# Delta rule's block stage: 16x16 diagonal blocks stored by eight transfers per tile, query products evicted by VectorE

## The chip, the cores and the metric

The kernel runs on one core of a Trainium2 chip. Its time is the device time of one execution in microseconds; a version's time is the median of its runs. The engines are TensorE (PE; its weight loads PEld), VectorE (DVE), ScalarE (ACT), GpSimd (POOL) and SyncE (SP), which issues most of the DMA transfers.

## What is computed

The reference is one inference step through two trunk layers of a hybrid backbone. The second layer holds a chunked gated delta rule. Of that the change touches the products and the inverses of small blocks:

```python
kb = kc * bc[..., None]
a_mat = jnp.where(strict, jnp.einsum('nbhid,nbhjd->nbhij', kb, kc) * gamma, 0.0) + jnp.eye(C_CHUNK)
sol = lax.linalg.triangular_solve(a_mat, rhs, left_side=True, lower=True)
attn = jnp.where(tri, jnp.einsum('nbhid,nbhjd->nbhij', qc, kc) * gamma, 0.0)
```

The kernel works on chunks of 128 tokens. The products of keys with keys (`kk`) and of queries with keys (`qk`) do not depend on the direction of the scan; gamma and beta do. The triangular system is solved by inverting its 16x16 diagonal blocks first and joining them later.

## The kernel before

`delta_net` (not far above the functions shown) runs four stages one after the other: `delta_prepare`, `delta_blocks`, `delta_chunks`, `delta_outputs`. Each is a `Stage` with its own buffers, and ends with a barrier of all engines. The change is in `delta_blocks` alone (its buffers are named `gdna_...` in the profile).

There are NT = 9 tiles of P = 128 tokens, 8 heads, blocks of BASE = 16, so NB = 8 blocks per tile. `delta_blocks` works as follows.

TensorE first turns the gates `gc` and `beta` (L2808, L2809). ScalarE copies them to `rows` (128 rows) and `rest` (16 rows), SyncE stores these four pieces (L2777, L2778), waits for them, and loads them back in another order as `gcb` and `bb` (L2781). Then for each tile t TensorE makes 8 products for `kk` into a PSUM tile `pk[t % 2]` and 8 for `qk` into `pq[t % 2]` (L2819). ScalarE evicts both (L2835), each a 128x1024 tile of 512 KB, into two alternating buffers of each. VectorE multiplies `kk` with a mask of the blocks, `own`, into `cut` (L2856), and sums over the blocks into `diag` (L2860), 128 rows by 8 heads by 16 columns: for each row only the 16 columns of its own block. SyncE's queue holds, tile after tile and in this order, the transfers of `diag` (L2784), `kk` (L2786) and `qk` (L2788) to scratch in HBM, each behind a wait for its producer.

Besides, after tile 2 VectorE subtracts `gcb` from itself across rows and columns into `E_` (L2863), and after tile 3 ScalarE makes the absolute value and the exponential of it (L2838, L2840).

When all of `diag` has landed (L2790), SyncE loads it back as `M` (L2792), in two halves, with one block of 16x16 in each partition and tile. VectorE multiplies it by `E_` (L2868) and by `bb` (L2871), inverts the blocks in 30 dependent steps of growing width (L2877, L2878), and makes the transpose `X` of the result (L2879). SyncE stores both as `inv` (L2797). The next stage, `delta_chunks`, reads `kk`, `qk` and `inv` back from HBM.

Transfers of other stages that the prediction looks at: `new_state` (L2961), four of 64 rows, each with four pieces of 256 B, strided at both ends; `moe_rowgp` (L2248), four in a row, of 32 rows of 1 KB; `front_cols` (L1141), of 64 rows of 4 B.

Of the kernel before, what the change touches and what calls it, by code (L numbers as in the profile page):

```python
# [10 lines left out]
ALU = mybir.AluOpType  # L11
ACT = mybir.ActivationFunctionType
AX = mybir.AxisListType

P = 128
# [5 lines left out]
NT = T // P  # L21
# [2547 lines left out]
HEADS = 8  # L2569
HALF = P // 2  # L2570
BASE = 16
NB = P // BASE
# [160 lines left out]

def own_block(a, own):

    return (a.rearrange("p h (b c) -> p h b c", c=BASE),
            own.rearrange("p (o b u) -> p o b u", o=1, u=1).broadcast_to([P, HEADS, NB, BASE]))


def delta_blocks(nc, io, keep, m):

    QT, KT, gc, beta, own = (m[x] for x in ("QT", "KT", "gc", "beta", "own"))
    with Stage(nc, "gdna") as s:
        kk = [s.sb(f"kk{i}", [P, HEADS, P]) for i in range(2)]
        qk = [s.sb(f"qk{i}", [P, HEADS, P]) for i in range(2)]
        cut = s.sb("cut", [P, HEADS, P])
        diag = [s.sb(f"diag{i}", [P, HEADS, BASE]) for i in range(2)]
        rows = s.sb("rows", [P, 2, P])  # L2750
        rest = s.sb("rest", [ROWS - P, 2, P])
        gcb = s.sb("gcb", [P, NT, BASE])
# [6 lines left out]
        pk = [s.ps(f"pk{i}", [P, HEADS, P]) for i in range(2)]  # L2759
        pq = [s.ps(f"pq{i}", [P, HEADS, P]) for i in range(2)]  # L2760
        row_turned, row_taken, row_out = s.sem("row_turned"), s.sem("row_taken"), s.sem("row_out")
        kk_mm, qk_mm, kk_taken, qk_taken = s.sem("kk_mm"), s.sem("qk_mm"), s.sem("kk_taken"), s.sem("qk_taken")
        cut_done, diag_done = s.sem("cut_done"), s.sem("diag_done")
        kk_out, qk_out, diag_out = ([s.sem(f"{n}{i}") for i in range(2)] for n in ("kk_out", "qk_out", "diag_out"))
        gcb_in, bb_in, M_in = s.sem("gcb_in"), s.sem("bb_in"), s.sem("M_in")
        E_done, E_step, Y_set, M_step, solve, inv_out = (s.sem(n) for n in ("E_done", "E_step", "Y_set", "M_step", "solve", "inv_out"))
        inv_done = s.sem("inv_done")
        blk = s.block()
        by_head = lambda a: a[:].rearrange("p (j r) i -> p r j i", r=2)
        by_bank = lambda a: a[:].rearrange("p (r j) i -> p r j i", r=2)  # L2770
        half = P // 2

        @blk.sync
        def _(sp):
            for i, name in enumerate(("gcT", "betaT")):
                sp.wait_ge(row_taken, i + 1)
                sp.dma_start(io[name][0:P, :], rows[:, i, :]).then_inc(row_out, 16)  # L2777
                sp.dma_start(io[name][P:ROWS, :], rest[:, i, :]).then_inc(row_out, 16)  # L2778
            sp.wait_ge(row_out, 64)
            for dst, name, done in ((gcb, "gcT", gcb_in), (bb, "betaT", bb_in)):  # L2780
                sp.dma_start(dst[:], io[name].rearrange("(t r) (b i) -> (r b) t i", t=NT, i=BASE)).then_inc(done, 16)  # L2781
            for t in range(NT):
                sp.wait_ge(diag_done, t + 1)
                sp.dma_start(io["diag"][t].rearrange("h p c -> p h c"), diag[t % 2][:]).then_inc(diag_out[t % 2], 16)  # L2784
                sp.wait_ge(kk_taken, t + 1)
                sp.dma_start(io["kk"][t], kk[t % 2][:]).then_inc(kk_out[t % 2], 16)  # L2786
                sp.wait_ge(qk_taken, t + 1)
                sp.dma_start(io["qk"][t], qk[t % 2][:]).then_inc(qk_out[t % 2], 16)  # L2788
            for i in range(2):
                sp.wait_ge(diag_out[i], 16 * len(range(i, NT, 2)))  # L2790
            for d in range(2):
                sp.dma_start(M[half * d:half * d + half].rearrange("p t i c -> p t (i c)"),  # L2792
                             io["diag"].rearrange("t h (b i) c -> (h b) t (i c)", i=BASE)).then_inc(M_in, 16)
            sp.wait_ge(inv_done, 1)
            for w, parts in enumerate(((X, Y), (Y, X))):
                for d in range(2):
                    sp.dma_start(io["inv"][w].rearrange("(t d h) (b i) c -> d (h b) t (i c)", t=NT, d=2, i=BASE)[d],  # L2797
                                 parts[d][half * d:half * d + half].rearrange("p t i c -> p t (i c)")).then_inc(inv_out, 16)
            for i in range(2):
                sp.wait_ge(kk_out[i], 16 * len(range(i, NT, 2)))  # L2800
                sp.wait_ge(qk_out[i], 16 * len(range(i, NT, 2)))
            sp.wait_ge(inv_out, 64)

# [18 lines left out]
        @blk.scalar  # L2822
        def _(act):
            for i in range(2):
                act.wait_ge(row_turned, i + 1)
                nc.scalar.activation(rows[:, i, :], pk[i][:, 0, :], ACT.Copy)
                nc.scalar.activation(rest[:, i, :], pk[i][0:ROWS - P, 4, :], ACT.Copy).then_inc(row_taken, 1)
            for t in range(NT):
                for dst, bank, mm, out, taken in ((kk, pk, kk_mm, kk_out, kk_taken), (qk, pq, qk_mm, qk_out, qk_taken)):
                    act.wait_ge(mm, t + 1)  # L2830
                    if t >= 2:
                        act.wait_ge(out[t % 2], 16 * (t // 2))
                        if dst is kk:
                            act.wait_ge(cut_done, t - 1)
                    nc.scalar.activation(by_head(dst[t % 2]), by_bank(bank[t % 2]), ACT.Copy).then_inc(taken, 1)  # L2835
                if t == 3:
                    act.wait_ge(E_done, 1)
                    nc.scalar.activation(E_[:], E_[:], ACT.Abs).then_inc(E_step, 1)  # L2838
                    act.wait_ge(E_step, 1)
                    nc.scalar.activation(E_[:], E_[:], ACT.Exp, scale=-1.0).then_inc(E_step, 1)  # L2840
# [8 lines left out]
        @blk.vector  # L2849
        def _(dve):  # L2850
            for t in range(NT):
                dve.wait_ge(kk_taken, t + 1)
                if t:
                    dve.wait_ge(diag_done, t)
                a, mask = own_block(kk[t % 2][:], own[:])
                nc.vector.tensor_tensor(cut[:].rearrange("p h (b c) -> p h b c", c=BASE), a, mask, ALU.mult).then_inc(cut_done, 1)  # L2856
                dve.wait_ge(cut_done, t + 1)
                if t >= 2:
                    dve.wait_ge(diag_out[t % 2], 16 * (t // 2))
                nc.vector.tensor_reduce(diag[t % 2][:], cut[:].rearrange("p h (b c) -> p h c b", c=BASE), axis=AX.X, op=ALU.add).then_inc(diag_done, 1)  # L2860
                if t == 2:
                    dve.wait_ge(gcb_in, 16)
                    nc.vector.tensor_tensor(E_[:], gcb[:].unsqueeze(3).broadcast_to([P, NT, BASE, BASE]),  # L2863
                                            gcb[:].unsqueeze(2).broadcast_to([P, NT, BASE, BASE]), ALU.subtract).then_inc(E_done, 1)
# [10 lines left out]
            for i in range(1, BASE):  # L2875
                p = prod[:, 0:NT * i * i].rearrange("p (t c j) -> p t c j", t=NT, c=i)
# [533 lines left out]
```

## Time and profile before

| | us |
|---|---|
| median of 3 runs | 4162.95 |
| the runs | 4156.73, 4162.95, 4169.68 |
| the profiled execution, its own time | 4168.26 |
| its span in the trace | 4166.5 |
| busy PE / DVE / ACT / POOL | 3579.7 / 2356.5 / 1697.6 / 580.3 |

The trace is of one execution. Times in it count from the start of the span. `delta_blocks` lies at about 2655 to 2762 us of it. "SPq" is SyncE's queue; the number beside one of its entries is the time that issuing the transfer took it, and the landing is told separately, in us from the issue to the last byte. A wait is written as the one who waits, an arrow, and who released it.

### The profile page before, as it was taken

To read this page: it belongs to the slowest core of one execution; us is meant where nothing else is said; L and a number is where in the kernel's file an instruction comes from. 1 tells how busy PE (TensorE), PEld (TensorE's weight loads), DVE (VectorE), ACT (ScalarE), POOL (GpSimd) and SP (SyncE) were. 2 spreads that over 40 slices of the span, in tenths; PEclk is the share of its full clock that TensorE was granted. 3 is DMA by queue.
4 is the path that set the end of the run, shared out by engine and by line. 5 is a ranking of instruction groups with operands and counts; after the bars stand their busy time and mean duration, and the time that the engine had idled before them with its cause. 6 is when DMAs were issued, how large, how long until landed. Compare 5 with 4: busy or idle time off the path is not lost. (4 is left out here: it accounts for less than half of the span.)

```text
span 4166.5 us, 56312 instructions
## 1 busy us (share of the span) xinstructions
PE 3579.7 (86%) x22440; PEld 2693.4 (65%) x22440; DVE 2356.5 (57%) x3625; ACT 1697.6 (41%) x2573; POOL 580.3 (14%) x467
## 2 busy tenths in 40 slices
PE   6979787997769999997999886439996689999995
PEld 1469755665646666664999764439995556666663
DVE  5163333334568787785514443645555668778884
ACT  2031154002346566563211266424434256656563
POOL 0020131221000010000200000026541101000000
PEclk8989898998879999998999997759997899999997
DMA  4142385414448888885443202333316458888885
GB/s 163 66 141 80 109 284 176 130 58 152 177 165 298 297 281 284 292 289 187 144 115 93 113 11 89 109 85 100 93 49 202 157 214 289 283 287 295 298 279 198
DMA packets 378504, 743.15 MB, mean 178 GB/s; under 512 B 99512, under 2 KB 222535, under 8 KB 377080
## 3 DMA queue, kind: packets, MB, share of 16 engines
q1 hardware_dynamic: 358906, 682.76, 47.2%
q0 software_dynamic: 16720, 56.41, 5.5%
q8 instruction: 178, 2.92, 0.3%
q10 hardware_dynamic: 2618, 0.40, 0.1%
q14 instruction: 82, 0.67, 0.0%
HBM read 634.01 MB, written 106.10 MB: 178 GB/s over the span
## 5 line engine op out<-in xcount | busy, mean ns | idle before, releaser
L2482 DVE TENSOR_TENSOR moe_w_low<-ffn_w,moe_w_high 128x1024 fp32r<-128x1024 f32 x768 | 898.9, 1220 | 77.0 <-ACT moe_w_high L2408 74.5
L2408 ACT ACTIVATE moe_w_high<-ffn_w 128x1024 fp32r<-128x1024 f32 x768 | 780.2, 1053 | 221.8 <-DMA ffn_w<-moe_w_gate 130.0
L2332 PE MATMUL moe_small<-ffn_w,ffn_xpT 128*16 128x512 f32 x2048 | 238.3, 594 | 0.0
L2312 PE MATMUL moe_G<-moe_w_high,moe_xT_high 128*128 128x512 f32 x512 | 185.4, 443 | 20.0 <-DVE moe_xT_low L2446 13.3
L224 PE MATMUL proj_mm<-proj_hT_low,proj_w_high 128*128 128x384 f32 x576 | 193.2, 335 | 0.0
L224 PE MATMUL proj_mm<-proj_hT_high,proj_w_low 128*128 128x384 f32 x576 | 193.1, 335 | 0.0
L224 PE MATMUL proj_mm<-proj_hT_high,proj_w_high 128*128 128x384 f32 x576 | 193.1, 335 | 0.0
L224 PE MATMUL proj_mm<-proj_w_high,proj_hT_high 128*128 128x416 f32 (+1 forms) x504 | 178.3, 354 | 11.7 <-POOL proj_hT_low L344 8.6
L3006 PE MATMUL gdnc_a<-gdnc_T,gdnc_kg 128*128 128x64 f32 (+1 forms) x864 | 102.1, 267 | 88.7 <-ACT gdnc_T L3056 86.5
L224 PE MATMUL proj_mm<-proj_w_high,proj_hT_low 128*128 128x416 f32 (+1 forms) x504 | 177.1, 351 | 0.0
L224 PE MATMUL proj_mm<-proj_w_low,proj_hT_high 128*128 128x416 f32 (+1 forms) x504 | 176.0, 349 | 0.0
L2261 POOL DMA_INDIRECT scratch_x<-moe_ys,keep_slot_s x32 | 50.5, 1579 | 867.3 <-DVE moe_ys L2475 867.3
L2312 PE MATMUL moe_Y<-moe_w_high,moe_hT_high 128*128 128x512 f32 x512 | 167.7, 409 | 0.0
L2312 PE MATMUL moe_G<-moe_w_low,moe_xT_high 128*128 128x512 f32 x512 | 161.9, 398 | 0.0
L2436 DVE TENSOR_SCALAR moe_xT<-moe_turn,keep_coef 128x128 f32<-128x128 f32 x248 | 84.8, 404 | 135.9 <-PE moe_turn L2288 135.9
L2312 PE MATMUL moe_G<-moe_w_high,moe_xT_low 128*128 128x512 f32 x512 | 160.0, 394 | 0.0
L2312 PE MATMUL moe_Y<-moe_w_low,moe_hT_high 128*128 128x512 f32 x512 | 159.9, 394 | 0.0
L2312 PE MATMUL moe_U<-moe_w_high,moe_xT_high 128*128 128x512 f32 x512 | 159.7, 393 | 0.0
L2312 PE MATMUL moe_Y<-moe_w_high,moe_hT_low 128*128 128x512 f32 x512 | 159.6, 393 | 0.0
L2312 PE MATMUL moe_U<-moe_w_low,moe_xT_high 128*128 128x512 f32 x512 | 159.3, 392 | 0.0
L2312 PE MATMUL moe_U<-moe_w_high,moe_xT_low 128*128 128x512 f32 x512 | 158.5, 391 | 0.0
L3006 PEld LDWEIGHTS gdnc_a<-gdnc_T,gdnc_kg 128*128 128x128 f32 (+1 forms) x864 | 92.9, 182 | 95.3 <-issue 93.9
(480 smaller groups left out, 7390.8 us busy)
## 6 DMA issues: line engine op xcount, KB each, us to landing
ffn_w<-moe_w_gate SPq DMA_DIRECT2D x256, 512.0 KB, 6.3
ffn_w<-moe_w_up SPq DMA_DIRECT2D x256, 512.0 KB, 7.1
ffn_w<-moe_w_down SPq DMA_DIRECT2D x256, 512.0 KB, 5.8
attnrun_m_w<-w_ada SPq DMA_DIRECT2D x40, 1024.0 KB, 11.3
scratch_conv<-proj_zf POOLq DMA_DIRECT2D x24, 512.0 KB, 2.9
scratch_tm<-proj_tm SPq DMA_DIRECT2D x45, 208.0 KB, 2.1
scratch_spec<-front_room SPq DMA_DIRECT2D x36, 256.0 KB, 2.1
proj_w_raw<-even_w_in SPq DMA_DIRECT2D x24, 384.0 KB, 4.2
```

The source lines that it names most:

```text
L224: mm = nc.tensor.matmul(out, lhs(a, k), rhs(b, k), start=first and n == 0, stop=last and n == len(passes) - 1)
L2261: nc.gpsimd.indirect_dma_start(out=io["x"][l], out_offset=bass.IndirectOffsetOnAxis(ap=rows, axis=0), in_=src[e % 2][:], in_offset=None, c ...
L2312: mm = nc.tensor.matmul(bank[:, half, :], stat[a][:, k, :], cut[b][:, half * BANK:(half + 1) * BANK], start=k == 0 and i == 0, stop=k == K ...
L2332: nc.tensor.matmul(out, stat, w, start=k == 0, stop=k == KD - 1, tile_position=(0, 32 * q)).then_inc(small_done, 1)
L2408: nc.scalar.activation(w_high[n % CUT_ROOM][:], raw_rows(wall, n), ACT.Copy).then_inc(w_up, 1)
L2436: ins = nc.vector.tensor_scalar(xT[:, k, :], turned(k, e), co[:, 0, k:k + 1], co[:, 1, k:k + 1], ALU.mult, ALU.add)
L2482: nc.vector.tensor_tensor(w_low[n % CUT_ROOM][:], raw_rows(wall, n), w_high[n % CUT_ROOM][:].bitcast(F32), ALU.subtract).then_inc(w_cut, 1)
L3006: mm = nc.tensor.matmul(quad(ba[hg])[later, h, :], kg[n % 3][:, 4 * hg + h, later], earlier(Tm[n % 2][:, 4 * hg + h, :], li, d), start=Tru ...
```

## The change

ScalarE evicts `kk` alone, and all nine tiles of it have room of their own. VectorE evicts `qk`, into two buffers as before, behind a wait for the transfer of two tiles earlier. The mask and the sum on VectorE are gone, and `cut` and `diag` with them. In place of the transfer of `diag`, SyncE issues eight transfers per tile straight from the evicted `kk`: for block b the 16 rows and, in each head, the 16 columns of the block, 16 rows of 8 pieces of 64 B. They stand ahead of the transfer of `kk` and wait for its eviction. All count on one semaphore, and `M` is loaded when all 72 have landed. ScalarE's two steps on `E_` stand after tile 4 in place of tile 3.

```diff
@@ def delta_blocks
-        kk = [s.sb(f"kk{i}", [P, HEADS, P]) for i in range(2)]
+        kk = s.sb("kk", [P, NT, HEADS, P])
         qk = [s.sb(f"qk{i}", [P, HEADS, P]) for i in range(2)]
-        cut = s.sb("cut", [P, HEADS, P])
-        diag = [s.sb(f"diag{i}", [P, HEADS, BASE]) for i in range(2)]
@@ SyncE
             for t in range(NT):
-                sp.wait_ge(diag_done, t + 1)
-                sp.dma_start(io["diag"][t].rearrange("h p c -> p h c"), diag[t % 2][:]).then_inc(diag_out[t % 2], 16)
                 sp.wait_ge(kk_taken, t + 1)
-                sp.dma_start(io["kk"][t], kk[t % 2][:]).then_inc(kk_out[t % 2], 16)
+                for b in range(NB):
+                    of_block = slice(b * BASE, (b + 1) * BASE)
+                    sp.dma_start(io["diag"][t, :, of_block, :].rearrange("h p c -> p h c"), kk[of_block, t, :, of_block]).then_inc(diag_out, 16)
+                sp.dma_start(io["kk"][t], kk[:, t]).then_inc(kk_out, 16)
                 sp.wait_ge(qk_taken, t + 1)
                 sp.dma_start(io["qk"][t], qk[t % 2][:]).then_inc(qk_out[t % 2], 16)
-            for i in range(2):
-                sp.wait_ge(diag_out[i], 16 * len(range(i, NT, 2)))
+            sp.wait_ge(diag_out, 16 * NB * NT)
@@ ScalarE
             for t in range(NT):
-                for dst, bank, mm, out, taken in ((kk, pk, kk_mm, kk_out, kk_taken), (qk, pq, qk_mm, qk_out, qk_taken)):
-                    act.wait_ge(mm, t + 1)
-                    if t >= 2:
-                        act.wait_ge(out[t % 2], 16 * (t // 2))
-                        if dst is kk:
-                            act.wait_ge(cut_done, t - 1)
-                    nc.scalar.activation(by_head(dst[t % 2]), by_bank(bank[t % 2]), ACT.Copy).then_inc(taken, 1)
-                if t == 3:
+                act.wait_ge(kk_mm, t + 1)
+                nc.scalar.activation(by_head(kk[:, t]), by_bank(pk[t % 2]), ACT.Copy).then_inc(kk_taken, 1)
+                if t == 4:
@@ VectorE
             for t in range(NT):
-                dve.wait_ge(kk_taken, t + 1)
-                if t:
-                    dve.wait_ge(diag_done, t)
-                a, mask = own_block(kk[t % 2][:], own[:])
-                nc.vector.tensor_tensor(cut[:].rearrange("p h (b c) -> p h b c", c=BASE), a, mask, ALU.mult).then_inc(cut_done, 1)
-                dve.wait_ge(cut_done, t + 1)
+                dve.wait_ge(qk_mm, t + 1)
                 if t >= 2:
-                    dve.wait_ge(diag_out[t % 2], 16 * (t // 2))
-                nc.vector.tensor_reduce(diag[t % 2][:], cut[:].rearrange("p h (b c) -> p h c b", c=BASE), axis=AX.X, op=ALU.add).then_inc(diag_done, 1)
+                    dve.wait_ge(qk_out[t % 2], 16 * (t // 2))
+                nc.vector.tensor_copy(by_head(qk[t % 2]), by_bank(pq[t % 2])).then_inc(qk_taken, 1)
```

## Rows read from the trace of the kernel before

**Rows 1.** The page: busy us of each engine, share of the span, instructions
```profile
PE 3579.7 (86%) x22440; PEld 2693.4 (65%) x22440; DVE 2356.5 (57%) x3625; ACT 1697.6 (41%) x2573; POOL 580.3 (14%) x467
```
**Rows 2.** Windows: stretch, its length, busy us by engine, PE clock, DMA share, GB/s
```profile
2661.00:2701.00 40.00, 17.45 (x250) 15.92 (x246) 29.72 (x19) 21.93 (x20) 0.44 (x1) 0.83 0.72 232
2701.30:2710.40 9.10, 0.00 (x0) 0.00 (x0) 0.00 (x0) 0.00 (x0) 0.00 (x0) 0.50 0.94 220
```
**Rows 3.** Waits from 2655 to 2765 us: us in total, times, longest
```profile
DVE gdna_M L2868 <- DMA gdna_M<-scratch_diag: 11.3, 1, 11.3
...
SPq L2784 <- DVE gdna_diag L2860: 25.9, 9, 5.2
```
**Rows 4.** Timeline, end of the loop: start, duration, engine, line, operation, [idle before]
```profile
2699.13 0.37 SPq L2784 DMA_DIRECT2D scratch_diag<-gdna_diag  x1
2699.55 0.58 SPq L2786 DMA_DIRECT2D scratch_kk<-gdna_kk  x1
2700.17 0.43 SPq L2788 DMA_DIRECT2D scratch_qk<-gdna_qk  x1
2701.32 1.70 SPq L2792 DMA_DIRECT2D gdna_M<-scratch_diag  x2
...
2710.41 2.56 DVE L2868 SCALAR_TENSOR_TENSOR gdna_M<-gdna_M,gdna_E 128x2304 f32<-128x2304 f32 x1 [11.30 <-DMA gdna_M<-scratch_diag]
```
**Rows 5.** Tiles cut, diag, qk: ns min/median/max, first and last start; last landing is qk's
```profile
L2856 DVE TENSOR_TENSOR gdna_cut<-gdna_kk,gdn_own x9: 1215/1225/1226, 2660.4 to 2696.0; 128x1024 f32<-128x1024 f32 x9
L2860 DVE TENSOR_REDUCE gdna_diag<-gdna_cut x9: 1857/1881/1923, 2661.7 to 2697.2; 128x128 f32<-128x1024 f32 x9
L2784 SPq DMA_DIRECT2D scratch_diag<-gdna_diag x9: 359/371/371, 2663.6 to 2699.1; - x9
...
L2835 ACT ACTIVATE gdna_qk<-gdna_pq x9: 1015/1024/1035, 2660.7 to 2696.3; 128x1024 f32<-128x1024 f32 x9
...
DMA to landing us min/median/max: 3.7/3.8/5.6
```
**Rows 6.** Line 2718: VectorE's copy from PSUM in the stage before
```profile
L2718 DVE COPY gdnp_q<-gdnp_bq x9: 679/679/692, 2605.0 to 2634.1; 128x512 f32<-128x512 f32 x9
```
**Rows 7.** Timeline of the steps on E_
```profile
2671.30 2.55 DVE L2863 TENSOR_TENSOR gdna_E<-gdna_gcb 128x2304 f32<-128x2304 f32 x1
...
2673.88 2.12 ACT L2838 ACTIVATE gdna_E<-gdna_E 128x2304 f32<-128x2304 f32 x1 [0.91 <-DVE gdna_E L2863]
...
2677.32 2.12 ACT L2840 ACTIVATE gdna_E<-gdna_E 128x2304 f32<-128x2304 f32 x1
```
**Rows 8.** Timeline of SyncE ahead of the loop, and the landings of rest
```profile
2657.19 0.33 SPq L2777 DMA_DIRECT2D scratch_gcT<-gdna_rows  x1
...
2658.04 0.41 SPq L2777 DMA_DIRECT2D scratch_betaT<-gdna_rows  x1
2658.50 0.43 SPq L2778 DMA_DIRECT2D scratch_betaT<-gdna_rest  x1
2659.96 0.37 SPq L2781 DMA_DIRECT2D gdna_gcb<-scratch_gcT  x1
2660.37 0.61 SPq L2781 DMA_DIRECT2D gdna_bb<-scratch_betaT  x1
...
DMA to landing us min/median/max: 1.4/1.4/1.4
```
**Rows 9.** Timeline of SyncE: four small transfers of the expert stage
```profile
1171.70 1.81 SPq L2248 DMA_DIRECT2D moe_rowgp<-scratch_mrow  x4
```
**Rows 10.** Tiles new_state and front_cols: issue ns min/median/max
```profile
L2961 SPq DMA_DIRECT2D new_state<-gdn_S x4: 612/617/638, 3070.9 to 3072.9; - x4
...
L1141 SPq DMA_DIRECT2D front_cols<-hy_b x4: 581/597/602, 2.2 to 5.4; - x4
```
**Rows 11.** Timeline: the first eviction of kk
```profile
2659.34 1.02 ACT L2835 ACTIVATE gdna_kk<-gdna_pk 128x1024 f32<-128x1024 f32 x1 [1.82 <-PE gdna_pk L2819]
```
**Rows 12.** DMA view, 2655 to 2760 us: GB/s in 40 equal slices
```profile
GB/s 0 56 62 72 358 346 158 340 46 384 0 234 297 318 239 297 314 261 283 204 126 0 0 0 0 3 0 0 0 0 0 0 0 0 0 0 161 219 238 262
```

More of the change, by code:

```diff
@@ L2732, in _ @@
                     nc.vector.tensor_tensor(y, y, ss[:, t, a, :].unsqueeze(2).broadcast_to([P, HEADS, HD]), ALU.mult).then_inc(scaled, 1)
-def own_block(a, own):
-    return (a.rearrange("p h (b c) -> p h b c", c=BASE),
-            own.rearrange("p (o b u) -> p o b u", o=1, u=1).broadcast_to([P, HEADS, NB, BASE]))
 def delta_blocks(nc, io, keep, m):
@@ L2762, in delta_blocks @@
         kk_mm, qk_mm, kk_taken, qk_taken = s.sem("kk_mm"), s.sem("qk_mm"), s.sem("kk_taken"), s.sem("qk_taken")
-        cut_done, diag_done = s.sem("cut_done"), s.sem("diag_done")
-        kk_out, qk_out, diag_out = ([s.sem(f"{n}{i}") for i in range(2)] for n in ("kk_out", "qk_out", "diag_out"))
+        kk_out, diag_out = s.sem("kk_out"), s.sem("diag_out")
+        qk_out = [s.sem(f"qk_out{i}") for i in range(2)]
         gcb_in, bb_in, M_in = s.sem("gcb_in"), s.sem("bb_in"), s.sem("M_in")
@@ L2768, in delta_blocks @@
         blk = s.block()
-        by_head = lambda a: a[:].rearrange("p (j r) i -> p r j i", r=2)
+        by_head = lambda a: (a[:] if a is qk[0] or a is qk[1] else a).rearrange("p (j r) i -> p r j i", r=2)
         by_bank = lambda a: a[:].rearrange("p (r j) i -> p r j i", r=2)
@@ L2798, in _ @@
                                  parts[d][half * d:half * d + half].rearrange("p t i c -> p t (i c)")).then_inc(inv_out, 16)
+            sp.wait_ge(kk_out, 16 * NT)
             for i in range(2):
-                sp.wait_ge(kk_out[i], 16 * len(range(i, NT, 2)))
                 sp.wait_ge(qk_out[i], 16 * len(range(i, NT, 2)))
```

## Prediction

> **What bounds the kernel now.** I began with the page: TensorE is busy for 86% of the span [rows 1]. That share is no guide here, because the change sits in one short stage, so I looked for that stage in the trace. Two windows describe it [rows 2]. From 2661.0 to 2701.0 us the nine tiles are multiplied, evicted and stored; no engine is busy throughout (VectorE 29.72 of 40 us, ScalarE 21.93, TensorE 17.45) and the DMA engines are busy for 72%. From 2701.3 to 2710.4 no compute engine does anything and the DMA share is 0.94.
>
> The stage's waits say what ends last [rows 3]. VectorE waits 11.3 us for `M` to be loaded from `diag`, and everything behind that wait is a serial chain on VectorE, then the transfers of `inv`, then the barrier. So one moment decides: when `M` has landed, 2710.41 us. It lands 9.1 us after SyncE issues it at 2701.32 [rows 4]. SyncE in turn was held by VectorE's `diag` nine times, 25.9 us in all [rows 3]. The nine transfers of `diag` start from 2663.6 to 2699.1 us [rows 5], 4.44 us a lap. Of that VectorE works 1.23 + 1.88 us on the mask and the reduce; the rest is waiting for `kk`, because ScalarE evicts both products, waits for buffers that are still being stored, and makes a detour over `E_`.
>
> **The change, part by part.** *Removed.* VectorE loses nine masks of 1.225 us and nine reduces of 1.881 us [rows 5], 28.0 us, and SyncE's 25.9 us of waiting on it go. What comes late next is not VectorE.
>
> *VectorE evicts `qk`.* The nearest row is its copy of 128x512 from PSUM, 679 ns [rows 6]; twice the width is at most 1.36 us, and the 1.02 us that ScalarE takes for the same tile [rows 5] is the other end. I take 1.36. It has the new wait on the transfer of `qk` two tiles back, whose slowest landing is 5.6 us [rows 5]. So a tile is evicted 5.6 + 1.36 = 7.0 us after that issue, and SyncE asks for it two laps later (9.5 us with the lap below): 2.5 us to spare. Behind this wait on VectorE stand the next evictions and the one subtraction for `E_`; on TensorE the product of `kk` for tile t+1 stands behind the product of `qk` for tile t, which needs the eviction of t-2, and that still leaves it two laps ahead of SyncE. Cost nothing; if the cover went, each us of late landing beyond 8.1 us would be paid in full once per two laps.
>
> *ScalarE evicts only `kk`,* into nine buffers, so it waits for no transfer. Its detour over `E_` (2673.88 to 2677.32 + 2.12 us, 5.6 us with a table load between [rows 7]) moves behind tile 4, where it waits for VectorE's subtraction of 2.55 us [rows 7]. That one follows tile 2's `qk`, whose buffer is free when tile 0's is stored: issued at about 2665.5, landed by 2669.3 (3.8 us, the median [rows 5]), evicted by 2670.6, subtracted by 2673.2. The detour ends at 2678.8, `kk` of tile 5 is evicted by 2680, and SyncE comes for it at 2661 + 5 x 4.76 = 2684.8. Cost nothing.
>
> *SyncE issues ten transfers per tile in place of three.* This is now the path: it has nothing to wait for, so the loop lasts as long as its issues. The trace of before holds no transfer of 16 rows by 8 pieces of 64 B. What it holds is how an issue's length depends on the one before it [rows 4]: behind `diag` (128 rows, 1,024 pieces) the issue of `kk` takes 0.58 us, behind `kk` (128 rows, 128 pieces) that of `qk` takes 0.43; gaps are 0.04. Call x what a small transfer costs its successor. A lap is 8x (seven small ones and `kk`) + 2 x 0.43 (`qk` and the next lap's first) + 10 x 0.044 = 8x + 1.30 us. The bounds for x, from three sorts of rows. At 0.41 to 0.43: behind `rest`, 16 rows, the next issue takes 0.41, and `rest` itself 0.43 [rows 8]; `moe_rowgp`, 32 rows each, goes four in 1.81 us, 0.46 from start to start [rows 9]. At 0.58: `diag` as it is, with the same eight pieces in a row [rows 4]. At 0.60 to 0.62: `new_state`, 64 rows of four pieces strided at both ends, 612 to 638 ns, and `front_cols`, 64 rows of 4 B, 597 ns [rows 10].
>
> I take 0.43. The new transfer has the row count of `rest` and the piece count of `kk` (128), and both give 0.41 to 0.43; the 0.58 stands behind eight times the pieces. The lap is 8 x 0.43 + 1.30 = 4.76 us by the unrounded 0.432.
>
> *Sum.* SyncE is free at 2660.37 + 0.61 + 0.04 = 2661.02 us [rows 8], when the first `kk` has been evicted (2659.34 + 1.02 = 2660.36 [rows 11]); the first issue is 0.17 longer behind `bb`. Nine laps of 4.76 are 42.8: SyncE reaches `M` at 2704.0. The last small transfer began 1.4 us earlier and lands 1.4 (`rest` [rows 8]) to 2.2 us (`diag`, 2699.13 to 2701.32 [rows 4]) after its start, so `M` is issued at 2704.0 to 2704.8; I take 2704.3. Its 9.1 us stay: `kk` and `qk` of the last tile lie ahead of it in the queue as now, only closer by 0.5 us, and those of the tile before are further gone; I allow 1 us either way. Against 2701.32 that is +3.0 us, and nothing later in the stage hides it. 4168.26 us of the profiled execution become 4171.3. That execution lay 5.3 us above the median of the three runs and inside their spread (4156.73 to 4169.68), so I put the same +3.0 on the median: 4166.0. With x = 0.41 the loop ends 1.6 us sooner (+1.4), with x = 0.50 it ends 4.9 us later (+7.9).
>
> **Rivals.** *Slow slots.* An issue's length might go with the shape and not with the pieces: `front_cols` has only 64 pieces and costs 0.60, so pieces alone don't order the rows. With x = 0.58 a lap is 5.94 us, nine are 53.5, +10.7 on the sum: +13.7 us, 4176.7. With 0.617 a lap is 6.24 and the sum +16.3: 4179.3. This decides the sign from x = 0.57 on. For it: `diag`, `new_state`. Against it: `rest` and `moe_rowgp`, the only ones with few rows. Chance 0.22.
>
> *Cheap issues.* If x were well under 0.41, data would bound the loop. A lap moves 2 x 524 KB + 66 KB = 1.11 MB; the two best neighbouring slices of the stage ran at 358 and 346 GB/s, a single one at 384 [rows 12]. At 352 a lap is 3.2 us, nine are 28.5, and with the last landing `M` is issued near 2692: -9 us, 4154. Even at 384 throughout it would be -12. No row has a store issued so fast. Chance 0.09. It is also the floor of the change: no case of mine reaches -12.5 us.
>
> *Small transfers hold the DMA engines.* `kk` and `qk` and the small pieces take 3.2 us of each lap's DMA time (72% of 4.44). If each small transfer kept the engines for a time of its own beyond its bytes, DMA would take over from SyncE at (4.76 - 3.2) / 8 = 0.2 us each, and every further 0.1 us would cost 9 x 8 x 0.1 = 7.2 us; at 0.6 us that is 29 us more, with the sum +32, 4195. Against it: four transfers of 64 and 8 KB begin at 2657.19 to 2658.50, the last two 0.46 us apart, `rest` lands in 1.4 us, and the wait for all four is over at 2659.96, 1.46 us after the last began [rows 8]. Chance 0.03.
>
> The Trainium skill speaks for that last rival: its page "DMA: Bandwidth & Descriptors", section "Bandwidth", calls transfers under 64 KB dominated by their descriptors and measures 0.68 us of DMA time for 4 KB beside 0.95 us for 64 KB, from GpSimd's queue. By it eight transfers of 8 KB would be an estimated 8 x 0.69 = 5.5 us of DMA time per tile in place of 0.95, 4.6 more; that is a lap of 7.8, and the time near 4195. The landings just named don't agree with adding them up.
>
> **How the numbers follow.** Forecast 0.66, slow slots 0.22, cheap issues 0.09, held engines 0.03. A measurement of this kernel can tell about 0.3%, 12.5 us, from no change. Over that on the slow side lie the held engines (0.03), most of the slow slots (0.16) and a little scatter: 0.20. On the fast side no case lies, only scatter, since the runs of before spread over 13 us: 0.03. Within: 0.77. The forecast with its bounds is 4164 to 4171; with the slow slots at the top, part of the cheap issues at the bottom and the scatter of a median of runs, 4157 to 4180.
>
> **What would show it.** In the changed profile: issues of `diag` about 0.43 us long, 0.48 from start to start, and `kk` behind them 0.43 and not 0.58; SyncE with no wait on VectorE, ScalarE or `qk` within the loop; the issue of `M` at the first small one's start plus 43 us, and 9 us on to VectorE's first use of `M`; VectorE's eviction of `qk` at 1.1 to 1.4 us. Wrong would be: small issues at 0.58 or more (slow slots), landings of small ones that grow from lap to lap (held engines), SyncE waiting for `qk_taken`, or an `M` that takes well over 10 us because the DMA queue is fuller than now.

## The result and the profile after

| | us |
|---|---|
| before, median of 11 runs (4156.73 to 4170.29) | 4164.6 |
| after, median of 11 runs (4169.33 to 4184.96) | 4177.81 |
| after / before | 1.0032, 95% interval 1.0023 to 1.0040 |
| the profiled execution of after, its own time / its span | 4184.96 / 4183.2 |

The change costs 13.2 us, 0.32%. That is inside the range of 4157 to 4180, but the sum had +3.0 us, and the result lies just beyond the bound of 0.3%. The stage accounts for all of it. I measure it from its first transfer (`gcT<-rows`) to VectorE's first use of `M`, behind which the chain is unchanged: 2710.41 - 2657.19 = 53.2 us before [rows 4, 8], and 67.2 us after, 14.0 more. The whole kernel's time scatters over 13 to 16 us from execution to execution, so the stage is the finer measure. Below, "stage time" is always this difference.

SyncE's timeline in after shows where they went. The columns are start, duration, engine, line, operation and count; the entries with x8 are the small transfers of one tile, merged. They answer to [rows 4] and [rows 8].

```profile
2656.88 0.33 SPq L2769 DMA_DIRECT2D scratch_gcT<-gdna_rows  x1
...
2660.07 0.61 SPq L2773 DMA_DIRECT2D gdna_bb<-scratch_betaT  x1
2660.72 4.86 SPq L2778 DMA_DIRECT2D scratch_diag<-gdna_kk  x8
2665.61 0.43 SPq L2779 DMA_DIRECT2D scratch_kk<-gdna_kk  x1
2666.09 0.44 SPq L2781 DMA_DIRECT2D scratch_qk<-gdna_qk  x1
2666.57 4.89 SPq L2778 DMA_DIRECT2D scratch_diag<-gdna_kk  x8
...
2678.31 5.59 SPq L2778 DMA_DIRECT2D scratch_diag<-gdna_kk  x8
...
2708.60 4.90 SPq L2778 DMA_DIRECT2D scratch_diag<-gdna_kk  x8
2713.54 0.43 SPq L2779 DMA_DIRECT2D scratch_kk<-gdna_kk  x1
2714.01 0.43 SPq L2781 DMA_DIRECT2D scratch_qk<-gdna_qk  x1
2714.60 2.06 SPq L2784 DMA_DIRECT2D gdna_M<-scratch_diag  x2
```

A lap is 5.88 us (2666.57 - 2660.72 = 5.85 for the first, 5.86 to 5.88 for five others), where the sum had 4.76. From the first small issue to `M` the loop takes 2714.60 - 2660.72 = 53.9 us, where the sum had 43.3. The stores of `kk` and `qk` cost 0.43 us each, as expected, but eight small ones take 4.86 to 4.90 us in seven of the nine laps (5.59 and 5.09 in the others) and not 8 x 0.43 + 7 x 0.044 = 3.75. The tile's groups (ns min/median/max) show that this isn't a general length: the median is 431 ns, the 0.43 of the sum.

```profile
L2778 SPq DMA_DIRECT2D scratch_diag<-gdna_kk x72: 303/431/2282, 2660.7 to 2713.1; - x72
L2842 DVE COPY gdna_qk<-gdna_pq x9: 1224/1225/1226, 2660.4 to 2705.9; 128x1024 f32<-128x1024 f32 x9
```

The last tile's first two small issues, from narrow windows of the timeline, show where the other 1.15 us sit:

```profile
2708.60 0.79 SPq L2778 DMA_DIRECT2D scratch_diag<-gdna_kk  x1
2709.43 1.20 SPq L2778 DMA_DIRECT2D scratch_diag<-gdna_kk  x1
```

They stand straight behind the stores of `kk` and `qk`. The first lasts 0.36 us longer than 0.43, the second 0.77, the third some 0.03, the rest no more. I call this excess the hold.

It is no wait for a producer. The waits view of SyncE's queue (total, times, longest) has only 1.7 us on ScalarE's eviction, once; before it had 25.9 us in nine waits [rows 3]. Even that one is none: it is put down to the small transfer issued at 2678.31, whose `kk` had been evicted by 2665.9, and whose issue lasted 2.28 us (more on it below). VectorE and ScalarE wait for others instead, and VectorE waits 17.0 us for `M` (11.3 before).

```profile
SPq L2778 <- ACT gdna_kk L2822: 1.7, 1, 1.7
...
DVE gdna_qk L2842 <- DMA scratch_qk<-gdna_qk: 32.7, 7, 6.4
DVE gdna_M L2850 <- DMA gdna_M<-scratch_diag: 17.0, 1, 17.0
```

The DMA engines are full during the hold and nearly idle behind it. In three whole laps (windows view; the last two columns are DMA share and GB/s) their share is 0.58, less than the 0.72 of before [rows 2]. But that is a mean. In the last lap it is 1.02 and 1.01 (a packet counts whole in the window in which it begins, hence more than 1) while the two held issues last, with the two big stores flowing at about 400 GB/s, and 0.16 once they are through:

```profile
2690.98:2708.60 17.62, 4.27 (x38) 3.68 (x34) 3.67 (x3) 1.02 (x1) 0.00 (x0) 0.50 0.58 190
2708.60:2709.40 0.80, 0.00 (x0) 0.00 (x0) 0.00 (x0) 0.00 (x0) 0.00 (x0) 0.50 1.02 404
2709.43:2710.63 1.20, 0.00 (x0) 0.00 (x0) 0.00 (x0) 0.00 (x0) 0.00 (x0) 0.50 1.01 403
2711.50:2712.50 1.00, 0.00 (x0) 0.00 (x0) 0.00 (x0) 0.00 (x0) 0.00 (x0) 0.50 0.16 17
```

The end of the stage, which answers to the last line of [rows 4]: `M` has landed 9.5 us after its issue, 9.1 before.

```profile
2724.10 2.56 DVE L2850 SCALAR_TENSOR_TENSOR gdna_M<-gdna_M,gdna_E 128x2304 f32<-128x2304 f32 x1 [16.95 <-DMA gdna_M<-scratch_diag]
```

### The profile page after: what moved, and what is told of

It reads as the page before. It is cut to its first block and busy times, and to the rows that moved or that the text cites. A ratio compares the mean times of both kernels' runs of the same rounds, so it can differ in the third digit from the quotient of the medians.

```text
span 4183.2 us, 56331 instructions
## 1 busy us (share of the span) xinstructions
PE 3588.8 (86%) x22440; PEld 2702.5 (65%) x22440; DVE 2338.2 (56%) x3616; ACT 1687.5 (40%) x2564; POOL 579.3 (14%) x467
## 5 line engine op out<-in xcount | busy, mean ns | idle before, releaser
L2261 POOL DMA_INDIRECT scratch_x<-moe_ys,keep_slot_s x32 | 50.5, 1579 | 866.1 <-DVE moe_ys L2475 866.1
## 6 DMA issues: line engine op xcount, KB each, us to landing
attnrun_m_w<-w_ada SPq DMA_DIRECT2D x40, 1024.0 KB, 11.8
```

Source lines behind the costliest of these rows:

```text
L2261: nc.gpsimd.indirect_dma_start(out=io["x"][l], out_offset=bass.IndirectOffsetOnAxis(ap=rows, axis=0), in_=src[e % 2][:], in_offset=None, c ...
```

## The experiments

My theory was that SyncE is held by what the two big stores have left queued, so that the hold belongs to `kk` and `qk` and neither to the small transfers nor to the evictions. The rivals were that VectorE's eviction is on the path, that the small transfers fill something themselves, and that the hold is a property of SyncE's own queue.

**The two halves of the change, apart.** First, ScalarE evicts `qk` again, with the small transfers kept:

```diff
@@ ScalarE, behind the eviction of kk
+                act.wait_ge(qk_mm, t + 1)
+                if t >= 2:
+                    act.wait_ge(qk_out[t % 2], 16 * (t // 2))
+                nc.scalar.activation(by_head(qk[t % 2]), by_bank(pq[t % 2]), ACT.Copy).then_inc(qk_taken, 1)
@@ VectorE
-                dve.wait_ge(qk_mm, t + 1)
-                if t >= 2:
-                    dve.wait_ge(qk_out[t % 2], 16 * (t // 2))
-                nc.vector.tensor_copy(by_head(qk[t % 2]), by_bank(pq[t % 2])).then_inc(qk_taken, 1)
```

> The changed kernel with the eviction of qk given back to ScalarE; the small transfers stay. Theory 1 (SyncE's issues are the loop: ten at 0.43 + 0.04 us, and once per lap a hold of some 1.1 us because kk and qk of the tile before, 1 MB, are still in the queue): the eviction is off the path, so the loop stays at 53.9 us from the first small transfer to the issue of M, and M lands 9.5 us later. Theory 2 (VectorE's waits for qk to land, 32.7 us in the trace of after, set the laps): the loop changes by more than 2 us, since ScalarE evicts in 1.02 and not 1.23 us and has its detour between.

One execution took 4187.17 us (before beside it: median 4162.23). Stage time 66.8 us, loop 53.5, lap 5.87: those of after. The eviction on VectorE neither costs nor brings anything here.

Second, the kernel before, with `qk` evicted by VectorE behind its mask and reduce, and nothing else:

```diff
@@ VectorE, behind the reduce
+                dve.wait_ge(qk_mm, t + 1)
+                if t >= 2:
+                    dve.wait_ge(qk_out[t % 2], 16 * (t // 2))
+                nc.vector.tensor_copy(by_head(qk[t % 2]), by_bank(pq[t % 2])).then_inc(qk_taken, 1)
@@ ScalarE
-                for dst, bank, mm, out, taken in ((kk, pk, kk_mm, kk_out, kk_taken), (qk, pq, qk_mm, qk_out, qk_taken)):
...
+                nc.scalar.activation(by_head(kk[t % 2]), by_bank(pk[t % 2]), ACT.Copy).then_inc(kk_taken, 1)
```

> The kernel before with only the other half of the change: VectorE evicts qk, mask, reduce and the one transfer of diag per tile stay. If a VectorE of 1.23 + 1.88 + 1.23 us per tile and 2.55 us once is the bound, the nine laps take at least 41.6 us in place of 37.7 (first diag issue to M issue) and M is issued 4 us later than before. If evicting with VectorE costs nothing because ScalarE gets free sooner, M is issued within 1 us of before. Nothing of the 13 us slower would come from here if the small transfers are the cause.

One execution took 4173.16 us. Stage time 55.9, 2.7 more than before (53.2). The six laps without the work on `E_` took 4.16 to 4.18 us (2660.98 to 2665.15 the first), where those of before took 3.24 to 4.56, 3.90 in the mean; the other two took 6.6 us each, where before they took 5.5 and 6.65, one of them with VectorE's subtraction of 2.55 us in it. So in this one execution VectorE's eviction looks to cost something while the mask and the reduce are still there. With them gone it costs nothing, as the run above shows. Of the 14.0 us nothing belongs to it, and the half of the change with the small transfers carries all of them.

**Where the hold stands.** `kk` goes between the fourth and the fifth small transfer, so that no two big stores are neighbours:

```diff
                     sp.dma_start(io["diag"][t, :, of_block, :].rearrange("h p c -> p h c"), kk[of_block, t, :, of_block]).then_inc(diag_out, 16)
-                sp.dma_start(io["kk"][t], kk[:, t]).then_inc(kk_out, 16)
+                    if b == 3:
+                        sp.dma_start(io["kk"][t], kk[:, t]).then_inc(kk_out, 16)
```

> The changed kernel with the same ten transfers per tile in another order: four small ones, kk, four small ones, qk. Theory 1 (the hold comes from 1 MB of kk and qk issued back to back ahead of the next small ones): there are 1.9 us of small issues between the two, the queue drains, the hold shrinks from 1.1 us to under 0.4 per lap; a lap goes from 5.9 to 4.8 to 5.1 us and the loop from 53.9 to 43 to 46. Rival (the hold belongs to the number of small transfers, one stall for every eight whatever stands between): the loop stays at 53 to 54 us.

One execution took 4175.76 us; stage time 64.5, loop 51.7, lap 5.49. The last lap on SyncE's timeline:

```profile
2705.51 2.24 SPq L2778 DMA_DIRECT2D scratch_diag<-gdna_kk  x4
2707.79 0.43 SPq L2780 DMA_DIRECT2D scratch_kk<-gdna_kk  x1
2708.26 2.23 SPq L2778 DMA_DIRECT2D scratch_diag<-gdna_kk  x4
2710.53 0.43 SPq L2782 DMA_DIRECT2D scratch_qk<-gdna_qk  x1
```

Four small ones without a hold would take 4 x 0.431 + 3 x 0.044 = 1.86 us. Each group takes 0.38 more. The hold follows the big stores, as the theory says, but I had expected less than 0.4 us of it per lap when they are apart, and a loop of 43 to 46 us. It only fell from 1.15 to 2 x 0.38 us: a miss in the size.

Then `kk` is stored behind the load of `M`, so that one big store per lap is left:

```diff
-                sp.dma_start(io["kk"][t], kk[:, t]).then_inc(kk_out, 16)
@@ SyncE, behind the load of M
+            for t in range(NT):
+                sp.dma_start(io["kk"][t], kk[:, t]).then_inc(kk_out, 16)
```

> The changed kernel with the nine transfers of kk issued behind M's load instead of in the loop. Theory 1: a lap has nine issues, 9 x 0.474 = 4.27 us, and with only 512 KB of qk ahead the hold nearly goes: loop 38.5 to 40 us in place of 53.9, M issued near 2700, and with one large transfer less ahead of it M lands in some 8 us: 2708, 16 us earlier than after and 2 earlier than before; the kernel near 4162, ratio to before 0.999. Rival (hold from the small ones): the loop is 38.4 + 9 x 1.1 = 48 us, the kernel some 5 us slower than before.

Median of 10 runs 4169.4 us, 1.0012 of before (1.0003 to 1.0022); stage time 57.2, loop 44.5. The end of the loop:

```profile
2701.13 4.12 SPq L2778 DMA_DIRECT2D scratch_diag<-gdna_kk  x8
2705.29 0.43 SPq L2780 DMA_DIRECT2D scratch_qk<-gdna_qk  x1
2706.35 1.31 SPq L2783 DMA_DIRECT2D gdna_M<-scratch_diag  x2
```

The hold is 4.12 - 3.75 = 0.37 us again, the lap 4.65. I had expected it to be nearly gone, a loop of 38.5 to 40 us and a ratio of 0.999. I had also expected `M` to land sooner, after 8 us, with half the stores ahead of it. It took 8.9 us (2706.35 to 2715.21), at a DMA share of 0.97.

```profile
2706.40:2715.20 8.80, 0.00 (x0) 0.00 (x0) 0.00 (x0) 0.00 (x0) 0.00 (x0) 0.50 0.97 248
```

Of the 2.18 MB that these 8.8 us moved only 1.18 are `M`'s; the rest are the stores of `kk` issued behind it. What `M` takes by itself shows the run on ScalarE's queue below.

**What a small transfer costs.** After, with eight further small transfers per tile into a part of `inv` that is overwritten later:

```diff
+                for b in range(NB):
+                    of_block = slice(b * BASE, (b + 1) * BASE)
+                    sp.dma_start(io["inv"][0, t * HEADS:(t + 1) * HEADS, of_block, :].rearrange("h p c -> p h c"), kk[of_block, t, :, of_block]).then_inc(diag_out, 16)
```

> The changed kernel with every small transfer issued a second time, into scratch that is written again later, so sixteen of them per tile. Theory 1 (a small transfer costs SyncE 0.43 + 0.04 us and nothing else; the hold of 1.15 us per lap belongs to kk and qk): a lap grows by 8 x 0.474 = 3.79 us to 9.7, the loop from 53.9 to 88 us, M lands 34 us later. Rival (a share of the hold belongs to the small ones, or they hold the DMA engines): the hold doubles too, a lap of 10.8 us and more, a loop of 98 us.

One execution took 4199.6 us; stage time 101.6 and loop 88.3, with 88 expected.

```profile
2725.02 4.89 SPq L2778 DMA_DIRECT2D scratch_diag<-gdna_kk  x8
2729.95 3.74 SPq L2781 DMA_DIRECT2D scratch_inv<-gdna_kk  x8
...
2696.04:2725.02 28.98, 2.08 (x16) 1.79 (x16) 3.67 (x3) 0.00 (x0) 0.00 (x0) 0.50 0.42 122
```

The second eight take 3.74 us, the price of the sum to the hundredth, and the first eight are held as in after. Small transfers of 128 pieces don't hold each other, sixteen in a row. The third line, a window of three whole laps, also prices them on the DMA engines: 0.42 x 28.98 / 3 = 4.06 us of DMA time per lap against 0.58 x 17.62 / 3 = 3.41 in after, so eight more cost 0.65 us, 0.08 each.

**Small transfers alone.** I first describe the order in which they are alone. TensorE makes all nine `kk`, then all nine `qk`; ScalarE evicts both; VectorE has only the subtraction; SyncE issues what `M` needs, then `M`, and behind it all stores of `kk` and `qk`. With this order and the 72 small transfers as in after:

```diff
@@ SyncE
             for t in range(NT):
                 sp.wait_ge(kk_taken, t + 1)
...
-                sp.dma_start(io["kk"][t], kk[:, t]).then_inc(kk_out, 16)
-                sp.wait_ge(qk_taken, t + 1)
-                sp.dma_start(io["qk"][t], qk[t % 2][:]).then_inc(qk_out[t % 2], 16)
@@ SyncE, behind the load of M
+            for t in range(NT):
+                sp.dma_start(io["kk"][t], kk[:, t]).then_inc(kk_out, 16)
+                sp.wait_ge(qk_taken, t + 1)
+                sp.dma_start(io["qk"][t], qk[t % 2][:]).then_inc(qk_out[t % 2], 16)
@@ TensorE
-            for t in range(NT):
-                for bank, src, done, taken in ((pk, KT, kk_mm, kk_taken), (pq, QT, qk_mm, qk_taken)):
+            for bank, src, done, taken in ((pk, KT, kk_mm, kk_taken), (pq, QT, qk_mm, qk_taken)):
+                for t in range(NT):
```

> The version with the products first, but with the 72 small transfers of the changed kernel, eight behind each eviction of kk, and no large transfer ahead of any of them. Theory 1 (the hold belongs to the large transfers): 72 issues at 0.474 us without a hold, 34.1 us from the first small transfer to the end of the last, M issued some 35 to 36 us after the first one, in place of 53.9. Rival (a hold once for every eight small ones): 44 us.

One execution took 4157.73 us, 2.7 below the median of before beside it (4160.47), which one execution can't tell from no change; stage time 50.3, against 67.2 in after. The single issues (x1) in these lines and in those of the next run are from narrow windows.

```profile
2647.48 36.78 SPq L2778 DMA_DIRECT2D scratch_diag<-gdna_kk  x72
...
2649.54 1.56 SPq L2778 DMA_DIRECT2D scratch_diag<-gdna_kk  x1
...
2663.48 1.60 SPq L2778 DMA_DIRECT2D scratch_diag<-gdna_kk  x1
...
2685.36 1.28 SPq L2781 DMA_DIRECT2D gdna_M<-scratch_diag  x2
```

Seventy-two at 0.474 us from start to start are 34.1 us. The other 2.7 are 0.17 in the first one, behind `bb` as predicted, and two single issues of 1.56 and 1.60 us, 1.13 and 1.17 too long. From the first issue to `M` it is 37.9 us; I had expected 35 to 36 without a hold, 44 with one. So the hold goes when the stores go.

The two long issues are something else. The DMA view has, in the whole stage, two packets of 16 KB of the kind "instruction" on a queue of their own, q8. The packets begin at 2649.30 and 2663.39, within 0.25 us of the start of these two issues. This line of the DMA view is of the window 2663:2665, around the second:

```profile
q8 instruction: 1, 0.02, 4.0%
```

In after they begin at 2662.22 and 2678.25, beside the issues of 1.37 us (2662.30, the first lap) and of 2.28 us (2678.31, the lap of 5.59). Every kernel here with the small transfers of 8 KB has such a pair, and each time an issue begun beside it is longer: by 0.9 to 1.2 us where nothing else holds it, by less where it falls into a hold. In before the two fell into SyncE's waits (2662.51 and 2675.67) and cost nothing. So the two moments go together; that the packet lengthens the issue is likely and was not tried. I put the first lap's 4.86 us, with no store of `kk` or `qk` before it, down to this and not to the hold. The loads of `gcb` and `bb` ahead of it (1,152 pieces of 64 B each) aren't ruled out by that issue alone, but the second one, with only small transfers ahead, is just as long.

**Whose queue it is.** ScalarE's queue carries the small transfers, SyncE's only `kk` and `qk`:

```diff
@@ SyncE
-                for b in range(NB):
...
@@ ScalarE, behind the eviction of kk
+                act.wait_ge(kk_taken, t + 1)
+                for b in range(NB):
+                    of_block = slice(b * BASE, (b + 1) * BASE)
+                    act.dma_start(io["diag"][t, :, of_block, :].rearrange("h p c -> p h c"), kk[of_block, t, :, of_block]).then_inc(diag_out, 16)
```

> The changed kernel with the 72 small transfers issued by ScalarE, eight behind each eviction of kk; SyncE issues only kk and qk. If the hold belongs to the queue on which the large transfers stand: ScalarE's lap is 1.02 + 8 x 0.474 = 4.8 us without a hold, and with the detour of 5.6 us the loop is 49 us from the first small transfer to M's issue, M landed 61 to 62 us after the stage's first transfer (67.2 in the changed kernel, 53.2 before). If it belongs to the DMA engines or to what both queues share: up to 10 us more, 59 and 71 us.

One execution took 4180.9 us; stage time 75.6, the longest but for the doubled one.

```profile
2704.10 0.32 SPq L2776 DMA_DIRECT2D scratch_kk<-gdna_kk  x1
...
2704.10 5.30 ACTq L2823 DMA_DIRECT2D scratch_diag<-gdna_kk  x8
2704.46 0.43 SPq L2778 DMA_DIRECT2D scratch_qk<-gdna_qk  x1
...
2704.96 1.02 ACTq L2823 DMA_DIRECT2D scratch_diag<-gdna_kk  x1
2706.01 1.40 ACTq L2823 DMA_DIRECT2D scratch_diag<-gdna_kk  x1
...
2709.45 1.02 ACT L2819 ACTIVATE gdna_kk<-gdna_pk 128x1024 f32<-128x1024 f32 x1 [5.38 <-issue]
```

Were the hold a matter of SyncE's own queue, ScalarE's eight issues would last 3.75 us and the stage 61 to 62. They last 5.30, on a queue that has no big store in it. That refutes a hold by the order within one queue. Nor does ScalarE wait for an issue of SyncE's in progress: the two held ones begin after SyncE's last was over (2704.46 + 0.43), while the DMA share is 1.01 and 1.03. The stage is longer still than after's because ScalarE's own work now stands in the same chain: the eviction of 1.02 us ("issue" in the last line; 5.30 + 1.02 + gaps is a lap of 6.4), and once the steps on `E_`, which make one lap 11.8 us (2679.49 to 2691.32).

Here the issue of SyncE's last store was over 5.6 us ahead of `M`'s, so `M` has the DMA engines to itself. It still takes 8.3 us, at 142 GB/s and a share of 0.71. So most of its landing is its own 1,152 pieces of 1 KB.

```profile
2716.88:2725.18 8.30, 0.00 (x0) 0.00 (x0) 0.01 (x1) 0.00 (x0) 0.00 (x0) 0.50 0.71 142
```

With four on each of the two queues (those of ScalarE on a semaphore of their own):

```diff
@@ SyncE
-                for b in range(NB):
+                for b in range(NB // 2):
@@ ScalarE, behind the eviction of kk
+                act.wait_ge(kk_taken, t + 1)
+                for b in range(NB // 2, NB):
...
```

> The changed kernel with blocks 0 to 3 issued by SyncE and blocks 4 to 7 by ScalarE. If a queue's issues are the bound, the work halves: SyncE's lap is 4 x 0.474 + 0.95 + a hold of 0.4 to 1.15 = 3.2 to 4.0 us, ScalarE's 2.9; nine laps are 29 to 36 us in place of 53.9, and M lands 43 to 50 us after the stage's first transfer, 3 to 10 us earlier than before; the kernel between 4151 and 4158. If the DMA engines were the bound, the loop would stay near 50 us.

Median of 10 runs 4159.35 us, 0.9999 of before (0.9988 to 1.0011); stage time 50.5. From SyncE's first small transfer to `M` the loop is 37.9 us (2657.53 to 2695.39), where I had expected 29 to 36: halving the issues per queue saves 16 us, not more, since the four of SyncE take 2.2 to 3.3 us in place of 1.86. The hold is there whichever queue issues. The Trainium skill says of this, on the page "DMA: Bandwidth & Descriptors", section "Issuing engines are not separate DMA queues", that issuing from several engines saves only the sequencer's time to issue. The trace agrees with that, but not with the page's word that this time is usually small beside the transfer: it was the bound here, and halving it is worth 16 us of the stage.

**Bytes or number of stores.** `kk` and `qk` of each tile are stored in halves, four heads in the loop and four behind the load of `M`. For the late half of `qk` the kernel stores `kk`'s again, so half of `qk` is left out; the sizes and the order are what counts here.

```diff
-                sp.dma_start(io["kk"][t], kk[:, t]).then_inc(kk_out, 16)
+                sp.dma_start(io["kk"][t, :, 0:4], kk[:, t, 0:4]).then_inc(kk_out, 16)
                 sp.wait_ge(qk_taken, t + 1)
-                sp.dma_start(io["qk"][t], qk[t % 2][:]).then_inc(qk_out[t % 2], 16)
+                sp.dma_start(io["qk"][t, :, 0:4], qk[t % 2][:, 0:4]).then_inc(qk_out[t % 2], 16)
@@ SyncE, behind the load of M
+            for t in range(NT):
+                for name in ("kk", "qk"):
+                    sp.dma_start(io[name][t, :, 4:8], kk[:, t, 4:8]).then_inc(kk_out, 16)
```

> The changed kernel with kk and qk stored in halves: in the loop only heads 0 to 3 of each (256 KB, the same 128 rows), the other half of kk behind M's load, and in place of the other half of qk that of kk, so that part of qk is wrong. Same number and order of transfers in a lap, half the bytes. If the hold goes with the bytes ahead: it falls from 1.15 us per lap to 0.4 or less, as behind one large transfer, and the loop from 53.9 to 43 to 47 us. If it goes with the number of transfers or rows: it stays at 53 to 54 us.

One execution took 4157.57 us; stage time 58.0, loop 45.7 (43 to 47 expected).

```profile
2683.28 0.43 SPq L2779 DMA_DIRECT2D scratch_kk<-gdna_kk  x1
2683.75 0.43 SPq L2781 DMA_DIRECT2D scratch_qk<-gdna_qk  x1
2684.23 3.81 SPq L2778 DMA_DIRECT2D scratch_diag<-gdna_kk  x8
```

Two stores of the same 128 rows, but of 256 KB each, leave 0.06 us of the hold. So at the same number of stores and rows it goes with how much they move. By size: 0.06 us behind two of 256 KB, 0.38 behind one of 512 KB, 1.15 behind two of 512 KB. The first two are the same 512 KB, so the total isn't all of it; in the first, half of it was issued 0.47 us earlier, and the pieces are half as long. These weren't varied apart.

**Fewer, larger small transfers.** The price of the stage is the number of issues ahead of `M`. A transfer of block b may carry all nine tiles, 16 rows of 72 pieces. First behind the loop of `qk`, with all of `kk` stored after the load of `M`:

```diff
@@ SyncE, in place of the loop over b; the loop over t holds only qk
+            sp.wait_ge(kk_taken, NT)
+            for b in range(NB):
+                of_block = slice(b * BASE, (b + 1) * BASE)
+                sp.dma_start(io["diag"][:, :, of_block, :].rearrange("t h p c -> p (t h) c"), kk[of_block, :, :, of_block].rearrange("p t h c -> p (t h) c")).then_inc(diag_out, 16)
```

> The changed kernel with eight transfers in all in place of 72: one per block, 16 rows of 72 pieces, for all nine tiles at once, behind the loop that stores qk; kk is stored behind M's load. The loop is then set by VectorE's evictions of qk and their landings, some 4.9 us per two tiles, and ends near 2682 us; eight issues of 0.6 us, landed near 2689, M landed near 2698 in place of 2724: 12 us earlier than before, ratio 0.997. Rival (what costs is the number of 64-byte pieces, 9,216 as before, and not the number of transfers): the eight take over 20 us and M lands no sooner than before.

Median of 10 runs 4154.67 us, 0.9988 of before (0.9978 to 0.9997), with 0.997 expected; stage time 45.6.

```profile
2652.27 21.39 SPq L2776 DMA_DIRECT2D scratch_qk<-gdna_qk  x9
2673.71 8.36 SPq L2780 DMA_DIRECT2D scratch_diag<-gdna_kk  x8
2684.45 1.28 SPq L2783 DMA_DIRECT2D gdna_M<-scratch_diag  x2
```

The eight cost 8.36 us, 1.05 each (7.55 in the next kernel, with nothing large ahead): an issue of 1,152 pieces is twice as long as one of 128, yet it replaces nine (I had expected 0.6 us each). Another 2.4 us pass until the last has landed (2673.71 + 8.36 = 2682.07 to 2684.45). Now the loop of `qk` is the largest part, 21.4 us, and `M` doesn't need it. So with the order of products described above, the stores of `qk` behind `M` too:

```diff
@@ SyncE, behind the load of M
             for t in range(NT):
+                sp.dma_start(io["kk"][t], kk[:, t]).then_inc(kk_out, 16)
                 sp.wait_ge(qk_taken, t + 1)
                 sp.dma_start(io["qk"][t], qk[t % 2][:]).then_inc(qk_out[t % 2], 16)
```

> A version that puts first what M needs: TensorE makes the nine tiles of kk ahead of those of qk, ScalarE evicts kk, then does its steps on E_, then evicts qk; SyncE issues the eight transfers of 16 rows by 72 pieces, M's load, and only then kk and qk of all tiles, beside VectorE's solve of 38 us. If the issues and the large transfers ahead are what M waits for: kk is evicted by 2670, M issued near 2677, landed near 2685, 25 us earlier than before; the kernel near 4138, ratio 0.994. Rival (M's landing is bound by something the order doesn't touch): less than 10 us gained.

Median of 5 runs 4140.88 us, 0.9959 of before (0.9945 to 0.9972); stage time 32.3, 20.9 less than before, where I had expected 25 less and 0.994. Two of the eight issues last 1.68 and 1.66 us (2662.99 and 2667.07, the fourth and the eighth), with no big store ahead and no packet of instructions beside, so transfers of 1,152 pieces do hold those behind them. The first wide issue waits until 2661.18 for the ninth `kk`, 12.4 us into the stage, while SyncE has nothing to do. Three tiles per transfer fill that time:

```diff
-            sp.wait_ge(kk_taken, NT)
-            for b in range(NB):
+            for g in range(0, NT, 3):
+                sp.wait_ge(kk_taken, g + 3)
+                for b in range(NB):
...
```

> The version with the products first, with the eight transfers made once for every three tiles (24 in all, 16 rows of 24 pieces), so that they start before the last tile is evicted. M was issued 23.8 us after the stage's first transfer with eight transfers in all; 24 issues of some 0.5 us starting 4 us earlier end near 19 us, M issued near 21, landed near 29.5 in place of 32.3: 23 us earlier than before, ratio 0.995. If issuing 24 costs more than starting sooner gives, it is no faster than with eight.

Median of 6 runs 4135.71 us, 0.9949 of before (0.9933 to 0.9965); stage time 28.4 (29.5 expected), 24.8 less than before and 38.8 less than after.

```profile
2655.97 13.10 SPq L2778 DMA_DIRECT2D scratch_diag<-gdna_kk  x24
2670.45 1.35 SPq L2781 DMA_DIRECT2D gdna_M<-scratch_diag  x2
```

The idea of the change, cutting the blocks by transfer and not by VectorE, is sound. It needs 24 issues and not 72, and it needs the large stores out of the way of `M`.

## Why the prediction was right and wrong

*The step that failed* is the size of the lap, in the paragraph on SyncE's ten issues: "it has nothing to wait for, so the loop lasts as long as its issues", each priced by the one before it. The first half held, the second didn't. I took an issue's length from its direct predecessor alone, and left out that it also depends on how much is still queued. The terms, from the timeline of after, in us against the sum's 43.3 for the loop: eight laps with a hold of about 1.12 (5.88 - 4.76), 9.0; the first lap, with the long issue beside the packet of instructions, 0.9 (5.85 - 4.76 - the 0.17 that I had allowed); two laps longer by a further 0.7 (the second such packet) and 0.2; less 0.2 of the wait for the last landing. Together 10.6, and 53.9 was measured. With `M`'s landing at 9.5 in place of 9.1 this is +14.0 in place of +3.0. The runs with `kk` moved (0.38 per store), with halves (0.06) and with the stores behind `M` (none) tie the 1.12 to the two big stores.

The trace of before had a hint: the two issues of `M` together took 1.70 us behind the stores of `kk` and `qk` [rows 4]. With only small transfers ahead they take 1.28. And in three laps of before the issue of `kk` took 0.69 to 0.71 us and not 0.58 (2667.27, for one), those whose first issue came only 2.2 to 2.4 us after the last store of the lap before. I had not asked why.

*x was right.* The choice between the bounds of 0.41 and 0.60 fell on 0.43; the median is 0.431, the doubled run confirms it at 3.74 us for eight.

*Slow slots* named nearly the right time (+13.7) from a wrong cause. By it each of the eight issues would last 0.58; most of them last 0.43, and the first two carry nearly all of the excess. It is only because of this rival that my range reached to 4180. That the measured 4177.8 lies in it is luck, and no explanation.

*Cheap issues* is refuted by the same median. *Small transfers hold the DMA engines* is refuted by the doubled run: 0.08 us of DMA time each, not 0.6. My estimate from the figures of the Trainium skill, page "DMA: Bandwidth & Descriptors", section "Bandwidth", was 4.6 us more DMA time for eight of them; the trace has 0.65.

*VectorE's eviction of `qk`* takes 1.225 us, between my 1.02 and 1.36, and costs nothing: with longer laps the cover grew. `qk` of the last tile was evicted from 2705.93 to 2707.2, and SyncE asked for it at 2714.01. *ScalarE's detour* was over at 2679.05 (2676.93 + 2.12; I had 2678.8) and costs nothing either. *VectorE's freed 28 us* bring nothing, as told: SyncE's issues took their place.

*The sign.* +3.0 was read as no change. With the lap at its true size the same working gives +14 and slower. So the path was right (SyncE's issues, with no wait), and one term of the sum was too small: the lap, by 1.12 us eight times over.

## What to carry to other kernels

Where a change turns compute work into transfers, count the issues on the path, at 0.43 us each here, before anything else: 72 of them cost more than the 28 us of VectorE's work that they replaced. An issue is no fixed cost. Look at whether its length grows behind large transfers, and keep large stores that nobody needs yet behind the small ones that somebody waits for. Widening each transfer over several tiles and ordering the work so that its input is ready early turned the same idea from +14 us into -25.

## What was unexpected of the hardware

- The issue of a transfer is held by what is still queued: 0.06 us behind two stores of 256 KB, 0.38 behind one of 512 KB, 1.15 behind two. The DMA engines are full while it lasts (share 1.0, about 400 GB/s), though their mean over these laps is 0.58.
- The hold is shared by both queues: eight issues on ScalarE's queue take 5.30 us while the stores are on SyncE's.
- The Trainium skill, page "Perfetto Trace Analysis", section "DMA Instruction — HWDGE (DVE, Sync)", says that an issue as profiled lasts until all of its descriptors have been generated (a descriptor tells a DMA engine of one piece to move) and the sequencer's own increments are made, and that a DMA engine may begin before, when more are generated than the buffer of descriptors holds. Both points above are compatible with a full buffer; no run here shows it. Bytes alone don't order the cases (one of 512 KB holds more than two of 256 KB, and the wide transfers of 72 KB hold too), nor do pieces alone (each big store has 128), and the two were not varied apart. That stays open.
- In every kernel with the small transfers of 8 KB two issues last longer than their kind, mostly by about 1 us (1.56 and 1.60 us in the run of small transfers alone), each beside a packet of 16 KB of the kind "instruction" on q8. Whether the packet is the cause, and whose instructions it brings, was not tried. It is 1.6 of the 14.0 us (0.9 in the first lap, 0.7 in the fourth).
- `M`'s load of 1.18 MB in pieces of 1 KB takes 8.3 us alone, at a DMA share of 0.71, and up to 9.5 behind other stores. In the stage of 28.4 us it is the second largest part, 8.5 us, behind the 24 issues with 13.1.
